# FFN gate of a two-layer trunk: silu as one activation in place of tanh and a product

## The reference

```
gate, up = _split(rms_norm(x, norm_ffn[i]) @ w_gate_up[i], (D_FF, D_FF))
x = x + (jax.nn.silu(gate) * up) @ w_down[i]
```

## Time and profile before

| What | Value |
| --- | --- |
| Median of three runs | 2149.47 us |
| Profiled execution, its own time | 2150.24 us |
| Span of the profile | 2148.5 us |
| TensorE (PE) busy | 2135.4 us, 99% |
| VectorE (DVE) busy | 1682.8 us, 78% |
| ScalarE (ACT) busy | 1119.4 us, 52% |
| GpSimd (POOL) busy | 56.6 us, 3% |
| Granted clock of TensorE | 1.0 in the mean |

### The profile page before, as it was taken

How to read it: one execution, slowest core, us unless ns; L and a number is a source line. 1 busy time by engine, 2 the same in 40 slices (tenths; PEclk the granted TensorE clock), 3 DMA queues, 4 the chain that set the end, 5 groups by cost and what they waited for, 6 DMA issues and landing times.

```text
span 2148.5 us, 29147 instructions
## 1 busy us (share of the span) xinstructions
PE 2135.4 (99%) x9992; PEld 1777.8 (83%) x9992; DVE 1682.8 (78%) x2139; ACT 1119.4 (52%) x1478; POOL 56.6 (3%) x99
## 2 busy tenths in 40 slices
PE   8999999999999999999999999999999999999999
PEld 7888888888888888888888888888888888888887
DVE  6657766898988898777666767667989898898775
ACT  7755654555455555454544544455554555555453
POOL 2101100000000000000000000000000000000000
PEclk9999999999999999999999999999999999999999
DMA  9765467667666766675665656577676667666664
GB/s 327 243 197 147 132 211 207 206 203 227 209 205 201 232 207 211 191 226 180 212 175 158 197 159 199 163 222 205 203 224 210 200 209 227 208 210 202 227 199 138
DMA packets 244568, 435.56 MB, mean 203 GB/s; under 512 B 23040, under 2 KB 43648, under 8 KB 244480
## 3 DMA queue, kind: packets, MB, share of 16 engines
q1 hardware_dynamic: 243392, 432.31, 65.1%
q10 hardware_dynamic: 1088, 2.10, 0.3%
HBM read 411.25 MB, written 2.10 MB: 192 GB/s over the span
## 4 chain that ended last, share of the span: by engine, by line
PE 99%; ACT 0%; DVE 0%; DMA 0%; issue 0%; DVEq 0%; SPq 0%; ACTq 0%
PE unit_bank L1886 30%; PE mix_bank L1928 24%; PE unit_bank L1928 24%; PE mix_bank L1898 7%; PE unit_bank L1898 7%; PE mix_bank L1886 4%; PE mix_bank L1979 1%; PE mix_bank L2109 1%; PE mix_bank L2044 0%; PE mix_bank L2006 0%; PE mix_bank L2053 0%; PE mix_bank L2095 0%; DVE w_lo L1104 0%; PE mix_bank L2017 0%; PE mix_bank L2028 0%; DMA source_T<-in_mem_T 0%
## 5 line engine op out<-in xcount | busy, mean ns | idle before, releaser
L644 ACT ACTIVATE w_hi<-raw 128x1024 fp32r<-128x1024 f32 x767 | 798.1, 1057 | 828.2 <-DVE sum_all L1128 166.5
L1104 DVE TENSOR_TENSOR w_lo<-raw,w_hi 128x1024 fp32r<-128x1024 f32 x767 | 923.4, 1221 | 353.0 <-ACT w_hi L644 346.8
L1886 PE MATMUL unit_bank<-w_hi,hT_hi 128*128 128x512 f32 (+1 forms) x576 | 181.2, 396 | 0.0
L1886 PE MATMUL unit_bank<-w_hi,hT_lo 128*128 128x512 f32 (+1 forms) x576 | 176.2, 387 | 0.0
L1886 PE MATMUL unit_bank<-w_lo,hT_hi 128*128 128x512 f32 (+1 forms) x576 | 175.9, 387 | 0.0
L1928 PE MATMUL unit_bank<-w_lo,hT_hi 128*128 128x512 f32 x480 | 147.9, 389 | 0.0
L1928 PE MATMUL mix_bank<-w_lo,hT_hi 128*128 128x512 f32 x480 | 147.8, 389 | 0.0
L1928 PE MATMUL mix_bank<-w_hi,hT_hi 128*128 128x512 f32 x480 | 147.8, 389 | 0.0
L1928 PE MATMUL unit_bank<-w_hi,hT_hi 128*128 128x512 f32 x480 | 147.8, 389 | 0.0
L1928 PE MATMUL unit_bank<-w_hi,hT_lo 128*128 128x512 f32 x480 | 147.8, 389 | 0.0
L1928 PE MATMUL mix_bank<-w_hi,hT_lo 128*128 128x512 f32 x480 | 147.7, 389 | 0.0
(11 more groups left out here) (427 smaller groups left out, 3602.7 us busy)
## 6 DMA issues: line engine op xcount, KB each, us to landing
raw<-in_w_gate_up SPq DMA_DIRECT2D x352, 512.0 KB, 4.4
raw<-in_w_down SPq DMA_DIRECT2D x176, 512.0 KB, 4.6
raw<-in_w_in_b SPq DMA_DIRECT2D x104, 512.0 KB, 3.7
raw<-in_w_o SPq DMA_DIRECT2D x64, 512.0 KB, 3.8
raw<-in_w_in_a SPq DMA_DIRECT2D x40, 512.0 KB, 3.7
moved<-turned SPq DMA_DIRECT2D x528, 32.0 KB, 2.5
raw<-in_w_mem_kv SPq DMA_DIRECT2D x31, 512.0 KB, 5.5
tanh_ff<-act_ff SPq DMA_DIRECT2D x112, 32.0 KB, 3.0
```

What stands on the lines that cost most here:

```text
L644: act.activation(w_hi[:, s, :, :], raw[:, r, :, :], ACT.Copy).then_inc(sems["hi_ready"], 1)
L1104: dve.tensor_tensor(w_lo[:, r, :, :], raw[:, r, :, :], w_hi[:, s, :, :].bitcast(F32), ALU.subtract).then_inc(sems["lo_ready"], 1)
L1886: ins = pe.matmul(all_banks[2 * pair + tile][:, 0:cols], stationary[part][:, kt + j, tile * P:(tile + 1) * P], b[:, j, 0:cols], start=open ...
```

## The change

The gate is taken by ScalarE's silu in one activation, with rs as the scale, and written over the gate sum in `act_ff`. VectorE's product (tanh + 1) * gate is gone, and with it the step `gate_silu` on VectorE. The product with the up part takes `act_ff` and rs in place of `tanh_ff` and rs * rs / 2, and waits for silu's signal. GpSimd's last product in `token_rs` is gone. The hunks left out rename the signal and drop a tile of two columns.

```diff
@@ -569,9 +568,7 @@
...
                 pool.tensor_tensor(dst[:, :], mean_sq[:, :], minus_half[:, 0:TILES], ALU.pow).then_inc(sems["pool_chain"], 1)
                 pool.wait_ge(sems["pool_chain"], t.next("pool_chain"))
-                pool.tensor_scalar(half_rs[:, :], dst[:, :], 0.5, 0.0, ALU.mult, ALU.add).then_inc(sems["pool_chain"], 1)
-                pool.wait_ge(sems["pool_chain"], t.next("pool_chain"))
-                pool.tensor_tensor(half_rs2[:, :], half_rs[:, :], dst[:, :], ALU.mult).then_inc(sems[ready], 1)
+                pool.tensor_scalar(half_rs[:, :], dst[:, :], 0.5, 0.0, ALU.mult, ALU.add).then_inc(sems[ready], 1)
 
             def heads(n, width):
...
@@ -933,11 +930,11 @@
...
                 x_sums(other, 3)
 
-                def gate_tanh():
+                def gate_silu():
                     for s in range(TILES):
                         act.wait_ge(sems["gate_sum"], t.next("gate_sum"))
-                        act.activation(tanh_ff[:, s, :], act_ff[:, s, :], ACT.Tanh,
-                                       scale=half_rs[:, s:s + 1]).then_inc(sems["tanh_ff_ready"], 1)
+                        act.activation(act_ff[:, s, :], act_ff[:, s, :], ACT.Silu,
+                                       scale=rs[:, s:s + 1]).then_inc(sems["silu_ready"], 1)
 
                 def chunk(j, shared):
...
@@ -946,7 +943,7 @@
...
                             sums_high(chunk_sums)
                         if i == 2:
-                            gate_tanh()
+                            gate_silu()
                         if i == 12:
                             act.wait_ge(sems["piece_used"], t.value("at"))
...
@@ -1574,20 +1571,12 @@
...
                 turn_x(other, 3, 1)
 
-                def gate_silu():
-
-                    for s in range(TILES):
-                        dve.wait_ge(sems["tanh_ff_ready"], t.next("tanh_ff_ready"))
-                        ins = dve.scalar_tensor_tensor(out=tanh_ff[:, s, :], in0=tanh_ff[:, s, :], scalar=1.0,
-                                                       in1=act_ff[:, s, :], op0=ALU.add, op1=ALU.mult)
-                    ins.then_inc(sems["dve_chain"], 1)
-
                 def times_up():
-                    dve.wait_ge(sems["dve_chain"], t.next("dve_chain"))
                     dve.wait_ge(sems["shared_free"], t.value("shared_free"))
                     for s in range(TILES):
+                        dve.wait_ge(sems["silu_ready"], t.next("silu_ready"))
                         ins = dve.scalar_tensor_tensor(out=up_ff[:, s, :], in0=up_ff[:, s, :],
-                                                       scalar=half_rs2[:, s:s + 1], in1=tanh_ff[:, s, :], op0=ALU.mult,
+                                                       scalar=rs[:, s:s + 1], in1=act_ff[:, s, :], op0=ALU.mult,
                                                        op1=ALU.mult)
                     ins.then_inc(sems["dve_chain"], 1)
...
@@ -1653,8 +1642,6 @@
...
                         if i + LEAD - 2 in SEVEN_PIECES:
                             sums_low(chunk_sums)
-                        if i == 4:
-                            gate_silu()
                         if i == 5:
                             times_up()
...
@@ -1729,8 +1716,6 @@
...
                 for p, (own, shared) in enumerate(chunk_banks):
                     for i in pieces(DOWN_PIECES, tail=layer == 1 and p == 1):
-                        if p == 0 and i == 2:
-                            gate_silu()
                         if p == 0 and i == 3:
                             times_up()
...
@@ -1760,9 +1745,9 @@
...
                 return {f"{k}{b}": n for b, n in enumerate(counts) if n for k in ("full", "free")}
 
-            per_chunks = slots(2 * CHUNK_PIECES) | {"tanh_ff_ready": 2 * TILES, "hi_block": 2 * TILES, "sum_ready": 2 * 3 * len(SEVEN),
+            per_chunks = slots(2 * CHUNK_PIECES) | {"silu_ready": 2 * TILES, "hi_block": 2 * TILES, "sum_ready": 2 * 3 * len(SEVEN),
                                                     "sum_hi_ready": 2 * len(SEVEN), "first_copied": 2, "own_free": 2,
-                                                    "shared_free": 2, "dve_chain": 2 * 4}
+                                                    "shared_free": 2, "dve_chain": 2 * 3}
 
 
```

More of the change, by code:

```diff
@@ L243, in trunk @@
         half_rs = keep("half_rs", [TILES])
-        half_rs2 = keep("half_rs2", [TILES])
         rs_mem = keep("rs_mem", [TILES])
@@ L377, in trunk @@
                "first_copied", "block_added", "down_form_ready", "gate_sum", "form_ready"]
-            + ["tanh_ff_ready", "tanh_q_ready", "tanh_gate_ready", "gate_used", "rung_ready", "early_ready"]
+            + ["silu_ready", "tanh_q_ready", "tanh_gate_ready", "gate_used", "rung_ready", "early_ready"]
             + ["dve_chain", "pool_chain"])
```

## The result

The changed kernel takes 2157.18 us (median of 7 runs, 2156.29 to 2157.90) against 2149.59 (7 runs, 2149.20 to 2150.74) for the kernel before: 7.6 us more, a ratio of 1.0034 with a 95% interval of 1.0023 to 1.0046. The forecast was 2157.0 with a range of 2152.5 to 2161.0. The profiled execution took 2157.18 us with a span of 2155.5, 7.0 us more than the span before. Two runs that lie far above all others of their kernel, 11170.83 us of the kernel before and 9381.25 us of one experiment, are left out of every comparison.

The account below looks back on a forecast made before the run. The prediction took TensorE, busy 2135.4 of 2148.5 us, to bound the kernel. Ten iterations at 0.75 us of new wait gave 7.5 us, all other terms 0: 2149.5 + 7.5 = 2157.0 us, range 2152.5 to 2161.0.

Parts of the forecast that it names:

- the place named: TensorE's first seven products of an FFN iteration (pieces 4 and 5): ten waits of about 0.7 us for a low half.
- The delay of split 5: ScalarE's split of piece 5, first chunk of an iteration: 1.41 us later through the table load ahead of the first silu.
- the rival of the double switch: Each table load also empties and refills ScalarE, costing 1.28 us more: 20 us in all, 2169.8 us; chance 0.05.
- Cover, latency, restart: At piece 5's low half: 0.68 us of slack, 0.06 us from VectorE to TensorE, 0.12 us recovered; 0.75 us lost per iteration.
- The loads that were priced at 0: Ten loads ahead of each iteration's first split, one ahead of layer 1's memory-attention exps: covered by idle time or slack, 0.
- The new wait: VectorE's product with the up sum now waits for silu itself: 6 us of cover, cost 0.
- 30 us less and nothing to show for it: VectorE loses 44 products of 686 ns, about 30 us, none on the path: gain 0.
- gain back VectorE's removed 1.3 us: Pieces behind the delayed low half recover 1.3 us because VectorE's product is gone, so no second stall follows.
- run beside the split ahead of it: Rival: the load ahead of silu overlaps split 4, nothing is left on the path, time stays 2149.5 us; chance 0.11.
- take two passes: Rival: each gate silu takes 1.42 us, delaying both chunks of an iteration: 30 us in all, 2179 us; chance 0.04.

Follow-up runs that it names:

- three loads: Changed kernel with a one-column silu and a one-column exp ahead of the gate's first silu in each iteration, so three table loads stand there: 2207.55 us against 2150.14.
- early silu: Changed kernel with both silu of a chunk and their table load moved on ScalarE ahead of the wait for the block sums: 2150.26 us against 2150.14.
- the product back: Changed kernel with two products of the removed shape put back on VectorE at the old steps, into an unread buffer: 2157.98 us against 2150.49.
- sixteen copies: Changed kernel with sixteen unread 128 x 64 copies on ScalarE between split 4 and the load, first chunk of each iteration: 2195.52 us against 2150.49.
- two copies: Changed kernel with two unread 128 x 512 copies on ScalarE between split 4 and the load, first chunk of each iteration: 2167.42 us against 2150.49.

## Why the prediction was right

*What bounds.* "What can move the time is a wait of TensorE that is not there now", and that is what came: ten waits at the place named, none in second chunks, and no other step between the pieces of the two traces.

*The delay of split 5.* Taken as 1.41 us from one load behind a busy ScalarE and the overlap that it ends; measured 1.43, of which 0.02 is silu being slightly longer than tanh over two tiles. The three loads in a row, 1.5 us from start to start with an activation of 0.20 us between them, show no second part either. So the rival of the double switch is out by the trace. The Trainium skill (ScalarE: Activation LUTs, section What ACT_TABLE_LOAD costs) prices a switch to another set at about 2.66 us, a load of 1283 ns and a drain of 1380 ns. The trace agrees with the load, 1.28 us in each of 24, and not with the drain: from split 4's end at 463.46 to silu's start at 464.78 are 1.32 us.

*Cover, latency, restart.* The cover was 0.68 to 0.69 us as read, the way from VectorE's end to TensorE's start 0.05 where 0.06 was taken, and 0.05 to 0.09 us is given back where 0.12 was taken: the 0.12 is there at the restart, ten times, but part of it is lost again within the seven products. 1.43 - 0.69 + 0.05 = 0.79, less about 0.07: 0.72 per iteration against 0.75. In the first iteration of each layer the cover is 0.78 us, a thing that the reading of one iteration missed, and the step 0.70, of which 0.61 is left. The ten add up to 7.0 in place of 7.5 us. The times differ by 7.6, 0.6 more than the spans of the two profiled executions, because the one before lay 0.65 us above its median and the one after on it. So the mechanism and its size are right, to half a microsecond; that 2157.0 lies only 0.2 us from the median of 2157.18 is luck, since the interval of the ratio is worth 4.9 to 9.9 us.

*The loads that were priced at 0.* At the loop's head 1.30 of 1.66 us of idle time were used up, with no effect. In layer 1 the last row of the exps in the changed kernel ends at 1073.09 and TensorE takes them at 1073.83, so 0.74 of the 2 us are left:

```profile
1072.88 0.21 ACT L739 ACTIVATION_READ_ACCUMULATOR p_b<-mix_bank,minus_max 128x1 f32 x1
...
1073.83 1.02 PEld L1964 LDWEIGHTS mix_bank<-ident,p_b 128*128 128x128 f32 x8
```

The early silu, with all 24 loads in place and no loss, shows it for the time.

*The new wait.* The second silu ends at 464.78 + 1.34 = 466.12 and the product with the up part starts at 472.58: 6.5 us of cover, where 6 were forecast.

*VectorE.* Forecast as 30 us less and nothing to show for it; 24.9 us less, and nothing to show for it against the kernel before. The 30 us are 44 times the length of one; busy time counts the moments in which two instructions overlap once, so it falls by less. The sentence that the pieces behind "gain back VectorE's removed 1.3 us" turned out to matter: with the product back they don't gain it, and piece 9 is late as well. The forecast had counted that relief as 0 and had used it in the same paragraph; its worth in the changed kernel, about 1 us, was not priced.

*The rivals.* The load does not run beside the split ahead of it: it starts 0.02 us after that split's end, ten times. Silu does not take two passes: 712 ns, where two would be 1.42 us.

## What to carry over

An activation of another function set is not one instruction: look in the built program for the table loads that come with it, above all at the head of a loop and ahead of the first such activation, and count them by executions. Price a load by the cover of what stands behind it on ScalarE: the same 1.28 us was free in an idle stretch and cost 0.7 us of the run behind a split that had waited for another engine. The remedy is to bring the set in once ahead of the loop, or to put the activation ahead of the wait instead of behind it; removing work from an engine that TensorE did not wait for was worth nothing by itself, and about 1 us where the load's delay had used up that engine's slack.

## What was not expected of the hardware

TensorE's granted clock fell to 0.5 at or just behind the end of a wait of 3.7 to 3.8 us in all ten iterations (three loads), and of one of 3.1 us in nine of ten (sixteen copies), but not at waits of 1.9 us (two copies) or 0.8 us (the changed kernel). It had been at 1.00 ahead of each of these waits, with matmuls without a pause. In the iterations shown it fell as the wait ended (sixteen copies: the first weight load is already slow) or about 0.5 us later (three loads: the first three, from 477.56, still take 0.19 us). With the slower matmuls behind it, a stall of 3.1 us cost 4.4 to 4.5 us, and one of 3.8 us between 5.1 and 6.4. All these waits are those of the weight loads; the matmuls stand idle 0.4 us less. With sixteen copies the first iteration of layer 0 kept its clock behind 3.05 us and the first of layer 1 lost it behind 3.06; with three loads, waits of the same 3.8 us were followed by a short or a longer stretch at the lower clock. What decides between the two levels is not told apart here.

No version tried is faster than the kernel before. The best with silu are level with it, at 1.0001.
